# Norm sums as columns of tokens, and roots spread from a repeated column, in a two-layer decoder trunk

## What is computed

```python
def rms_norm(x, g):
    y = x * lax.rsqrt(jnp.mean(x * x, axis=-1, keepdims=True) + EPS)
    return y * g

def layer_norm(x, g, b):
    mu = jnp.mean(x, axis=-1, keepdims=True)
    var = jnp.mean(jnp.square(x - mu), axis=-1, keepdims=True)
    return (x - mu) * lax.rsqrt(var + EPS) * g + b

for l in range(2):
    h = modulate(rms_norm(x, norm1_g[l]), sh1, sc1)
    y = conv_gmlp_mixer(h, ...) if l == 0 else short_conv_mixer(h, ...)   # layer 0 holds two layer_norms
    x = x + g1 * y
    h = modulate(rms_norm(x, norm2_g[l]), sh2, sc2)
    x = x + g2 * peer(h, ...)
return rms_norm(x, final_g)
```

## Time and profile before

| what | value |
|---|---|
| time, median of 3 runs | 2862.64 us (2861.79 to 2863.04) |
| span of the profiled execution, first to last instruction (the profile gives no other time for it) | 2861.6 us |
| PE busy | 2815.2 us, 98% of the span |
| DVE busy | 2321.0 us, 81% |
| ACT, POOL busy | 1200.4 us and 1199.7 us, 42% each |
| chain that ended last, by engine | PE 92%, DVE 6%, DMA 1% |
| granted TensorE clock, mean | 0.996 of full speed |

### The profile page before, as it was taken

One profiled execution on the slowest core, in us unless ns is written; L12 is line 12 of the kernel. 1 busy time (PEld: TensorE's weight loads), 2 busy tenths in 40 slices (PEclk: granted clock), 3 DMA queues, 4 the chain that ended last, 5 costly groups with the idle time before them and its releaser, 6 DMA issues.

```text
span 2861.6 us, 46635 instructions
## 1 busy us (share of the span) xinstructions
PE 2815.2 (98%) x15014; PEld 2496.4 (87%) x15014; DVE 2321.0 (81%) x4531; ACT 1200.4 (42%) x1602; POOL 1199.7 (42%) x790
## 2 busy tenths in 40 slices
PE   7999999999999999999999999999999999999998
PEld 5767999999999888888878789999999988888886
DVE  6995799979994888888864608999899858888887
ACT  3443443346663333333332424333566533333333
POOL 2623488873336222222134345888533532222221
PEclk8999999999999999999999999999999999999999
DMA  6446578899999999999844234988999989999995
GB/s 267 144 141 255 201 273 286 293 322 351 366 387 327 343 344 350 341 348 346 317 169 172 76 104 156 318 288 291 308 386 372 372 323 343 349 344 347 346 341 206
DMA packets 301610, 830.70 MB, mean 290 GB/s; under 512 B 29856, under 2 KB 134432, under 8 KB 300832
## 3 DMA queue, kind: packets, MB, share of 16 engines
q1 hardware_dynamic: 180368, 469.57, 46.5%
q0 software_dynamic: 73728, 268.47, 26.3%
q10 hardware_dynamic: 47376, 90.88, 8.3%
HBM read 731.80 MB, written 96.99 MB: 290 GB/s over the span
## 4 chain that ended last, share of the span: by engine, by line
PE 92%; DVE 6%; DMA 1%; ACT 0%; issue 0%; POOL 0%; SPq 0%; DVEq 0%; ACTq 0%
PE bank L1631 12%; PE bank L1633 12%; PE bank L1632 12%; PE bank L1684 12%; PE bank L1685 12%; PE bank L1686 12%; PE bank L1504 4%; PE bank L1505 4%; PE bank L1506 4%; PE bank L1653 3%; DVE rows L1362 2%; PE bank L1609 1%; DVE shared L950 1%; DMA shared<-mod_rows 1%; PE bank L1520 0%; PE bank L1524 0%
## 5 line engine op out<-in xcount | busy, mean ns | idle before, releaser
L626 ACT ACTIVATE w_hi<-w_raw 128x1024 fp32r<-128x1024 f32 x342 | 361.7, 1058 | 666.5 <-PE bank L1686 655.3
L1684 PE MATMUL bank<-w_hi,h_hi 128*128 128x512 f32 x1536 | 597.7, 389 | 0.0
L1686 PE MATMUL bank<-w_lo,h_hi 128*128 128x512 f32 x1536 | 597.6, 389 | 0.0
L1685 PE MATMUL bank<-w_hi,h_lo 128*128 128x512 f32 x1536 | 597.6, 389 | 0.0
L1631 PE MATMUL bank<-h_hi,w_hi 128*128 128x384 f32 x1376 | 462.9, 336 | 0.0
L1633 PE MATMUL bank<-h_lo,w_hi 128*128 128x384 f32 x1376 | 459.9, 334 | 0.0
L1632 PE MATMUL bank<-h_hi,w_lo 128*128 128x384 f32 x1376 | 459.7, 334 | 0.0
L1232 DVE TENSOR_TENSOR w_lo<-w_raw,w_hi 128x1024 fp32r<-128x1024 f32 x256 | 313.9, 1226 | 179.2 <-ACT w_hi L626 179.2
L1684 PEld LDWEIGHTS bank<-w_hi,h_hi 128*128 128x128 f32 x1536 | 288.3, 188 | 60.7 <-issue 0.8
L1686 PEld LDWEIGHTS bank<-w_lo,h_hi 128*128 128x128 f32 x1536 | 288.3, 188 | 59.8
L1685 PEld LDWEIGHTS bank<-w_hi,h_lo 128*128 128x128 f32 x1536 | 288.3, 188 | 59.7
(11 more groups left out here) (237 smaller groups left out, 5318.3 us busy)
## 6 DMA issues: line engine op xcount, KB each, us to landing
w_raw<-stream SPq DMA_DIRECT2D x600, 512.0 KB
act_dram<-act_words ACTq DMA_DIRECT2D x248, 192.0 KB
act_words<-act_dram SPq DMA_DIRECT2D x248, 192.0 KB, 5.0
gate_dram<-shared ACTq DMA_DIRECT2D x80, 512.0 KB
shared<-gate_dram SPq DMA_DIRECT2D x64, 640.0 KB
oh_words<-mod_rows SPq DMA_DIRECT2D x60, 512.0 KB, 4.9
oh_ic<-mod_rows SPq DMA_DIRECT2D x20, 512.0 KB, 5.6
shared<-mod_rows SPq DMA_DIRECT2D x16, 512.0 KB, 14.9
```

Of the source, the lines that this page charges most:

```text
L626: nc.scalar.activation(hi_of(grp, s), w_raw[:, s, :], ACT.Copy).then_inc(S["hi_ready"], 1)
L1684: MM(o, p_hi, hi, start=start, stop=False)
L1685: MM(o, p_lo, hi, start=False, stop=False)
L1686: ins = MM(o, p_hi, lo, start=False, stop=stop)
```

## The change

The squares become the stationary operand and one column of ones the moving one, so that a sum lands as a column with tokens on the partitions, 128 tokens at a time: four matmuls of one column for each block of squares (`column_sums`), in place of one of 512. `take_diagonal` goes. `inverse_roots` reads the 128x4 sums from PSUM and is rewritten with nine operations instead of eleven; its last one raises `diag_ready`. The product with the identity (L934) and `stat` go too: `spread_roots` now takes a root column repeated 128 times as the stationary operand and the identity as the moving one, four matmuls of 128 columns. `keep_busy` makes two matmuls after the sums instead of four. At norm 2 POOL makes `add_squares` ahead of the low part of tile 1 instead of behind it. The sums of a layer norm's mean stay as they were.

```diff
-                    if name == "od_in" and s == 2:
+                    if name == "od_in" and s == 1:
                         add_squares(2, 0)
...
-            def take_diagonal(m, bank, width):
-                for b in range(TB):
-                    ins = V.scalar_tensor_tensor(out=stat[:, 2 + m, b * P:(b + 1) * P],
-                                                 in0=ps[bank][:, b * P:(b + 1) * P], scalar=1.0 / width, in1=ident[:],
-                                                 op0=ALU.mult, op1=ALU.mult,
-                                                 accum_out=var_c[:, m * TB + b:m * TB + b + 1])
...
+            def inverse_roots(m, bank, width):
+                v, r, t = (c[:, m * TB:(m + 1) * TB] for c in (var_c, root_c, root_t))
+                link(V.tensor_scalar(v, ps[bank][:, 0:TB], 1.0 / width, EPS, ALU.mult, ALU.add))
+                link(V.tensor_scalar(r.bitcast(I32), v.bitcast(I32), -0.5, float(0x5F1FFFF9), ALU.mult, ALU.add))
...
-                for m in norms:
-                    ins = V.tensor_tensor(stat[:, m, :].rearrange("p (b t) -> p b t", t=P),
-                                          ident[:].unsqueeze(1).to_broadcast([P, TB, P]),
-                                          root_c[:, m * TB:(m + 1) * TB].unsqueeze(2).to_broadcast([P, TB, P]), ALU.mult)
-                    ins.then_inc(S["diag_ready"], 1)
+                V.scalar_tensor_tensor(out=r, in0=t, scalar=1.875 / kept, in1=r, op0=ALU.add, op1=ALU.mult
+                                       ).then_inc(S["diag_ready"], 1)
...
+            def column_sums(bank, src, start, stop):
+                for b in range(TB):
+                    ins = MM(ps[bank][:, b:b + 1], src[:, b * P:(b + 1) * P], ones[:, 0:1],
+                             start=(start and b == 0), stop=(stop and b == TB - 1))
+                return ins
...
-                MM(ps[bank][:], ones[:], stat[:, m, :], start=True, stop=True).then_inc(S["inv_ready"], 1)
+                for b in range(TB):
+                    ins = MM(ps[bank][:, b * P:(b + 1) * P], root_c[:, m * TB + b:m * TB + b + 1].to_broadcast([P, P]),
+                             ident[:], start=True, stop=True)
+                ins.then_inc(S["inv_ready"], 1)
...
-                keep_busy(4)
+                keep_busy(2)
```

More of the change, by code:

```diff
@@ L917, in inverse_roots @@
[L917 to L924, removed]
+            def inverse_roots(m, bank, width):
+                v, r, t = (c[:, m * TB:(m + 1) * TB] for c in (var_c, root_c, root_t))
+                link(V.tensor_scalar(v, ps[bank][:, 0:TB], 1.0 / width, EPS, ALU.mult, ALU.add))
+                link(V.tensor_scalar(r.bitcast(I32), v.bitcast(I32), -0.5, float(0x5F1FFFF9), ALU.mult, ALU.add))
+                outer, inner, kept = 0.703952253, 2.38924456, 0.375
@@ L925, in inverse_roots @@
                 link(V.tensor_tensor(t, r, r, ALU.mult))
-                link(V.scalar_tensor_tensor(out=t, in0=t, scalar=-outer, in1=v, op0=ALU.mult, op1=ALU.mult))
-                link(V.scalar_tensor_tensor(out=r, in0=t, scalar=outer * inner, in1=r, op0=ALU.add, op1=ALU.mult))
-                link(V.tensor_tensor(t, r, r, ALU.mult))
+                link(V.scalar_tensor_tensor(out=t, in0=t, scalar=-outer * kept, in1=v, op0=ALU.mult, op1=ALU.mult))
+                link(V.scalar_tensor_tensor(out=r, in0=t, scalar=outer * inner * kept, in1=r, op0=ALU.add,
+                                            op1=ALU.mult))
@@ L939, in norm_root @@
+                V.scalar_tensor_tensor(out=r, in0=t, scalar=1.875 / kept, in1=r, op0=ALU.add, op1=ALU.mult
+                                       ).then_inc(S["diag_ready"], 1)
             def norm_root(n):
                 dve.wait_ge(S["ssum"], n + 1)
-                link(take_diagonal(0, 5, D))
-                inverse_roots(range(1))
+                inverse_roots(0, 5, D)
             def norm_dve(n, gain_col, shift):
@@ L967, in ln_root @@
                 dve.wait_ge(S["ln_mm"], 2 * m + 2)
-                link(take_diagonal(m, sq_bank[m], AC * P))
-                inverse_roots(range(m, m + 1))
+                inverse_roots(m, sq_bank[m], AC * P)
             def ln_scale(m, src, gain_name):
@@ L1544, in projections_and_squares @@
                 pe.wait_ge(S["sq_sum"], (RESIDUAL.index(n) + 1) * (KC - 3))
[L1545 removed]
+                column_sums(5, sq[:, 0, :], True, False)
                 pe.wait_ge(S["sq_ready"], n * KC + KC - 1)
[L1547 removed]
+                column_sums(5, sq[:, KC - 2, :], False, False)
                 pe.wait_ge(S["sq_ready"], (n + 1) * KC)
[L1549 removed]
+                column_sums(5, sq[:, KC - 1, :], False, True).then_inc(S["ssum"], 1)
                 spread_busily(n)
+            def column_sums(bank, src, start, stop):
[3 more added lines that the diff above has]
+                return ins
             def square_sum(n, k):
                 pe.wait_ge(S["sq_ready"], n * KC + k + 1)
[L1554 removed]
+                ins = column_sums(5, sq[:, k, :], k == 0, k == KC - 1)
                 if k == KC - 1:
@@ L1583, in sum_shared_squares @@
                     pe.wait_ge(S["sq_ready"], n * KC + k + 1)
-                    MM(ps[5][:], ones[:], sq[:, k, :], start=(k == POOL_SQUARES), stop=False)
+                    column_sums(5, sq[:, k, :], k == POOL_SQUARES, False)
                 pe.wait_ge(S["sq_pool"], (l + 1) * (POOL_SQUARES - 1))
-                MM(ps[5][:], ones[:], sq[:, 0, :], start=False, stop=True).then_inc(S["ssum"], 1)
+                column_sums(5, sq[:, 0, :], False, True).then_inc(S["ssum"], 1)
                 spread_busily(n)
@@ L1595, in ln_sum, with ln_square_sum @@
                     ins.then_inc(S["ln_mm"], 1)
+            def ln_square_sum(m):
+                for c in range(AC):
+                    pe.wait_ge(S["ln_sqd"], m * AC + c + 1)
+                    ins = column_sums(sq_bank[m], ln_sq[m][:, c, :], c == 0, c == AC - 1)
+                ins.then_inc(S["ln_mm"], 1)
             def peer_pe(l):
```

11 lines of the change are left out of this document (4 added, 7 removed).

## The result

| | us |
|---|---|
| before, median of 21 runs | 2862.63 (2861.68 to 2863.65) |
| after, median of 21 runs | 2866.81 (2862.85 to 2868.47) |
| ratio | 1.0013, 95% interval 1.0007 to 1.0019 |
| predicted | 2859.5 (2852.5 to 2864.0) |
| profiled execution of after, and its span | 2868.39, 2866.6 |

The kernel became slower, by 4.2 us at the medians. That is less than the 0.2% that the prediction took a measurement to tell from no change; the interval of 21 runs each lies just above 1. The time lies outside the predicted range, and the trace shows a large loss beside a large gain.

What follows compares the result with a forecast made beforehand. PE's dense matmuls hold most of the chain; at norms the PE-DVE root path bounds it. Terms +1.4 - 1.1 - 1.1 - 2.05 + 0.9 - 2.05 + 0.9 = -3.1 gave 2859.5 us, range 2852.5 to 2864.

Steps and rivals of the forecast that it cites:

- The root path: From sums to scaling at a norm: diagonal, two operations and identity product removed, 3.0 instead of 5.07 us, 2.05 less.
- The pass: One-column pass of the sums: 0.11 us at full clock, 0.213 at half clock.
- norm 0: Start, at half clock: 64 passes take 13.65 us, DVE goes on 1.4 us late, delaying the first projection.
- the rival built on it: A pass costs 0.107 us at half clock too: norm 0 gains 1.9 us, total 2856.2; chance 0.04.
- LN 0: First layer norm: the new root still meets POOL's low part and waits; 1.1 us less, 3.15 if it escapes.
- LN 1: Second layer norm: mixing matmuls ahead of the spread end at 164.6, so the spread gains only 1.1 us.
- Norms 1 and 3: Stretch of about 2.8 us without wide matmuls is too short for a clock fall; each gains 2.05 us.
- Norms 2 and 4: Clock falls within the sums, at 1437.4 to 1438.2 in norm 2; each becomes 0.9 us longer.
- POOL at norm 2: POOL's low parts hold DVE's second root operation until 1441.6, taking the whole 2.05 us gain unless DVE slips in between.
- The rival "the clock holds": No clock fall in norms 2 and 4: -7.0 us, 2855.7, or 2851.6 if DVE also escapes POOL; chance 0.32.

Runs made afterwards that it cites:

- experiment 1: The changed kernel with 128 equal columns of ones moving through each block of squares instead of one: 2854.07 us, ratio 0.9967.
- experiment 9: Experiment 1's kernel with POOL's low parts and LN 1's spread reordered, 128 columns moving in the start's shift passes, fillers around them: 2851.09 us; two more fillers, 2845.59.

## Why the prediction was wrong, point by point

**The root path** was right. Nine operations took 1.74 us instead of the earlier trace rows's 2.16 for eleven, the diagonal and the product are gone, and from sums to scaling 3.0 us pass where the clock holds (2.99 in experiment 1).

**The pass** was right at both clocks. At norm 1 twenty-four passes took 2.65 us in the chain, 0.110 each; in norm 0, with the sums of the start at half clock, they took 0.215:

```profile
10.70 13.78 PE L1536 MATMUL bank<-ones,shared 128*128 128x1 f32 x64 [10.70 <-ACT shared L641]
28.18 10.24 PE L1716 MATMUL bank<-c_col,shared 128*128 128x1 f32 x48
```

```profile
24.52 0.16 DVE L909 TENSOR_SCALAR var_c<-bank 128x4 f32<-128x4 f32 x1 [3.22 <-PE bank L1536]
```

13.78 / 64 = 0.215, and DVE waited 3.22 us for it, as was said. The rule of the Trainium skill, page "TensorE: Matmul & The Clock Gate", section "LDWEIGHTS (loading the stationary operand)", columns over 1.2 GHz, 0.107 us for 128 with no word of the clock gate, does not give the 0.215 of this form here; the rival built on it falls. (The clock column is no evidence in this stretch: in this trace it reads 1.00 up to its first change, at 127.54, while these passes take twice their time.) The first projection came 0.74 us late and its input 0.43 early (10.70 against 11.13), 1.2 in all, against 1.4 predicted.

**LN 0.** The step that DVE meets POOL was right as a mechanism (2.32 us in experiment 1, 136.31 to 138.63) and wrong for this run. Here the clock had already fallen in the layer norm's own sums. ACT waited 9.42 us for PE's bank, where it waited 6.04 in before, made its high part late, and POOL's low part came after the root:

```profile
139.82 2.39 POOL L488 TENSOR_TENSOR w_lo_first<-w_raw,w_hi_first 128x1024 fp32r<-128x1024 f32 x1 [8.62 <-ACT w_hi_first L625]
```

```profile
136.46 0.15 DVE L909 TENSOR_SCALAR var_c<-bank 128x4 f32<-128x4 f32 x1
156.66 2.48 DVE L945 SCALAR_TENSOR_TENSOR shared<-bank,shared 128x512 f32<-128x512 f32 x4 [3.86 <-PE bank L1584]
```

```profile
143.44 1.05 PE L1551 MATMUL bank<-ident,root_c 128*128 128x128 f32 x8
```

The root escaped, and this stage became 3.43 us shorter instead of 1.1. But PE, slowed by the clock, spread only at 143.44, 2.5 us later than in before, and behind the convolution's steps (L1343) DVE waited 3.86 us for PE's sums of the mean of LN 1, where it waited 1.29. Most of the gain was taken back by LN 1's scaling. I had counted DVE as the bound and had not asked whether PE would hold its clock there.

**LN 1** was forecast 1.1 us shorter and came out 2.8 longer. Its mixing, ahead of the spread, ran in part at half clock (the last three mixings and the spread's start lie 4.4 us apart, 161.66 to 166.05, and 2.7 in experiment 1, 161.00 to 163.68), and the spread came no earlier: 166.05 against 165.83.

**Norms 1 and 3: the step that failed.** The prediction took 3.9 and 4.7 us, the two delays between the last wide matmul and a fall that the trace of before happened to hold, as the shortest that can occur, and so called a stretch of 2.8 us safe. In the trace of after the clock falls at 127.54, 161.67, 216.29, 1434.85, 1625.99 and 2847.96 (worked out from the mean clock of the stretches in which it falls), and the delays, counted from the end of the last matmul of 128 or more columns, are 3.6, 4.0, 3.0, 2.3, 2.0 and 2.8 us. Norm 1 kept 0.8 of its 2.05 us, norm 3 lost 0.9 instead. Two observed values were used as a bound, and the range was not widened for it. For LN 0 and LN 1, with 32 such passes each, the sum had no term of the clock at all. The stages of the traces add up to +5.0 us against the forecast's -3.1: of the 8.1 between them norms 1 and 3 hold 4.2, norms 2 and 4 3.0, LN 0 and LN 1 together 1.6, and norm 0 takes 0.7 off.

**Norms 2 and 4** had the mechanism right and a term too small. The clock was to fall at about 1437.8, 1.2 us ahead of the end of the sums. It fell at 1434.85, 1.1 us into the passes. The sums then took 7.69 us and not 5.6, and the stage became 2.4 us longer and not 0.9. The fillers ended after the root, as forecast; the spread took 1.19 us at norm 2, the clock returning within it, and 1.68 at norm 4.

**POOL at norm 2** was to hold the root until 1441.6. Its low parts ended at 1440.5, ahead of a root that the clock had made late; in experiment 1 the operation that meets them lasts 1.86 us, against 2.1 forecast.

**The rival "the clock holds"** was worked out to -7.0 us. Experiment 1, the nearest to it that was run, gave -9.0 at the medians, and most of the difference is norm 0: its first projection came 0.44 us earlier and not 1.4 later, since with 128 columns moving the sums take 9.62 us for 64 passes and not 13.78, a pace at which part of them must have run at full clock. The range's upper end failed for the same reason as the forecast: it allowed for a worse clock in two norms and not in all six places.

## What to carry to other kernels

When a change replaces wide matmuls by ones of few columns, look for the granted clock in each place where they run; that an engine reads as fully busy is no evidence that it keeps its clock, and moving 128 columns instead of one cost less than 0.01 us per pass here. Two observed delays are not a bound. Work put in to bridge a wait must end before the wait does, at the lower clock too; otherwise it is the wait.

## What the runs showed of the hardware that was not expected

- Passes that load 128 columns of weights and move one column leave PE 2.00 of 2.00 us busy and see the clock fall 2.0 to 4.0 us after the last matmul of 128 or more columns; with 128 columns moving the clock stayed at 1.00 in the same places. The pass itself costs nearly the same: the 24 passes of norm 1 take 2.91 us wide and 2.81 narrow, both at full clock.
- When the clock rises in the start differs by 3 us between two executions of kernels alike up to there (43.1 and 46.2 us), and LN 0's root lies 1.5 us apart. Once the clock held throughout, in experiment 9, five runs lay within 0.42 us.
- A DVE operation of 128x4 elements that meets two POOL operations of 2.33 us each in a row lasts until both are done (1.86 us instead of 0.17), and one of 128x512 with two SBUF operands is held too (2.08 instead of 0.74); one with its second operand in PSUM isn't (0.69).
